# Two steps of a chunked recurrence at a time between the weight tiles of a projection

## The reference

```
z = rmsnorm(h); q, f, i, og, pool, gates = split(z @ w_in)
f = lb + (1 - lb) * sigmoid(f);  k = 1 - f;  a = cumsum(log f) in a chunk
o_inter = (q * exp(a)) @ S                      # S: state of the head, 128 x 64
scores[t, s] = sum_k q[t] * exp(a[t] - a[s]) * k[s],  s <= t
o = o_inter + scores @ v
S = exp(a_last) * S + (k * exp(a_last - a))^T @ v
```

## Time and profile before

| | us |
|---|---|
| median of 3 runs | 1472.34 |
| profiled execution, its own time | 1473.41 |
| span of the profile | 1471.6 |
| TensorE matmuls busy | 1451.9 |
| VectorE busy | 828.5 |
| ScalarE busy | 691.1 |
| GpSimd busy | 161.6 |

### The profile page before, as it was taken

One profiled execution on the slowest core, in us unless ns is written; L12 is line 12 of the kernel. 1 busy time (PEld: TensorE's weight loads), 2 busy tenths in 40 slices (PEclk: granted clock), 3 DMA queues, 4 the chain that ended last, 5 costly groups with the idle time before them and its releaser, 6 DMA issues.

```text
span 1471.6 us, 26477 instructions
## 1 busy us (share of the span) xinstructions
PE 1451.9 (99%) x11311; PEld 1284.0 (87%) x11311; DVE 828.5 (56%) x1335; ACT 691.1 (47%) x1025; POOL 161.6 (11%) x308
## 2 busy tenths in 40 slices
PE   7999999999999999999999999999999999999998
PEld 7999989999999898998888777788899888778888
DVE  6487867764656556654335787642223566644343
ACT  6475877853443222322233676642222777743232
POOL 0025400000000000000000044300000233320000
PEclk9999999999999999999999999999999999999999
DMA  7222121123422223222334333433223333342222
GB/s 238 94 66 89 63 83 59 59 73 137 131 94 86 87 87 113 87 87 82 106 101 108 63 47 20 77 94 109 86 86 89 68 71 71 72 105 93 86 94 79
DMA packets 138968, 130.24 MB, mean 89 GB/s; under 512 B 26569, under 2 KB 134884, under 8 KB 138596
## 3 DMA queue, kind: packets, MB, share of 16 engines
q1 hardware_dynamic: 134084, 120.39, 26.0%
q0 software_dynamic: 4752, 8.16, 5.3%
q10 hardware_dynamic: 16, 0.00, 0.0%
HBM read 119.69 MB, written 4.26 MB: 84 GB/s over the span
## 4 chain that ended last, share of the span: by engine, by line
PE 91%; DVE 3%; ACT 3%; issue 1%; DMA 0%; SPq 0%; DVEq 0%; ACTq 0%
PE PS L962 79%; PE PS L1288 3%; PE PS L1261 2%; PE PS L1244 2%; DVE wlo L1937 1%; PE PS L1248 1%; PE PS L1247 1%; PE PS L1073 1%; ACT L1439 1%; ACT whi L1439 0%; DMA xt<-in_x 0%; ACT Pm L1439 0%; PE PS L1129 0%; PE PS L1029 0%; DVE zlo L1985 0%
## 5 line engine op out<-in xcount | busy, mean ns | idle before, releaser
L962 PE MATMUL PS<-zhi,whi 128*128 128x258 f32 (+2 forms) x1856 | 486.9, 320 | 3.2 <-ACT qf L1439 1.0
L962 PE MATMUL PS<-zhi,wlo 128*128 128x258 f32 (+2 forms) x1856 | 476.8, 314 | 0.0
L962 PE MATMUL PS<-zlo,whi 128*128 128x258 f32 (+2 forms) x1856 | 475.4, 314 | 0.6 <-DVE zlo L1985 0.6
L962 PEld LDWEIGHTS PS<-zhi,whi 128*128 128x128 f32 x1856 | 306.9, 189 | 27.9 <-issue 2.6
L962 PEld LDWEIGHTS PS<-zhi,wlo 128*128 128x128 f32 x1856 | 305.6, 189 | 22.3
L962 PEld LDWEIGHTS PS<-zlo,whi 128*128 128x128 f32 x1856 | 305.5, 189 | 20.8 <-DVE zlo L1985 0.8
L1937 DVE TENSOR_TENSOR wlo<-raw,whi 128x2048 fp32r<-128x2048 f32 (+2 forms) x114 | 249.3, 2187 | 121.5 <-ACT whi L1439 121.4
L1439 ACT ACTIVATE whi<-raw 128x2048 fp32r<-128x2048 f32 (+2 forms) x114 | 207.4, 1820 | 150.4 <-DMA raw<-in_w_up 55.2
L1439 ACT ACTIVATE Pm<-Pm,small 128x144 f32<-128x144 f32 (+3 forms) x128 | 73.1, 571 | 38.6 <-DVE small L2467 38.3
L2467 DVE CUSTOM_DVE_ANT_0 Pm<-PS,cmask 128x144 f32<-128x144 f32 (+3 forms) x128 | 62.9, 503 | 35.8 <-PE PS L1244 21.5
L962 PE MATMUL PS<-glo,whi 128*128 128x512 f32 x176 | 69.9, 397 | 0.0
(11 more groups left out here) (357 smaller groups left out, 2171.4 us busy)
## 6 DMA issues: line engine op xcount, KB each, us to landing
raw<-in_w_in SPq DMA_DIRECT2D x50, 1024.0 KB, 5.3
raw<-in_w_up SPq DMA_DIRECT2D x22, 1024.0 KB, 5.1
raw<-in_w_out SPq DMA_DIRECT2D x8, 1024.0 KB, 5.2
raw<-in_w_down SPq DMA_DIRECT2D x8, 1024.0 KB, 5.3
raw<-in_w_br_mla SPq DMA_DIRECT2D x4, 1024.0 KB, 5.1
raw<-in_w_br_fox SPq DMA_DIRECT2D x4, 1024.0 KB, 5.1
raw<-in_w_down SPq DMA_DIRECT2D x4, 768.0 KB, 4.3
hspill<-hT SPq DMA_DIRECT2D x1, 2112.0 KB, 7.6
```

The lines of the kernel that those rows point to most:

```text
L962: ins = mm(o_, l_, r_, start=first, stop=last)
```

## The change

Three things. On TensorE, steps 1, 3 and 5 of a pair are not done behind their own weight tile but kept in a list `held`, and done with the next entry of the order that does not itself end in such a step; on that occasion the held step and the entry's own follow each other. The update of chunk c goes to columns 128 c to 128 c + 127 of bank 7, so only the update of chunk 2 still waits for a state. On VectorE, `state(c)` waits for the updates of both steps of a couple, and reads the new columns; of the two places where differences and state were taken ahead, the one for i = 3 (in the f tile with i = 2) stays and the one for i = 4 goes back to its own entry.

```diff
@@ TensorE, step
-                        else:
-                            pe.wait_ge(s_ready, 4 * p + c)
+                        elif c == 2:
+                            pe.wait_ge(s_ready, 4 * p + 2)
                         for hh in range(2):
                             h = 2 * p + hh
+                            u0 = P * c + 64 * hh
                             for r in range(0, P, 32):
-                                ins = mm(PS[r:r + 32, 7, 64 * hh:64 * hh + 64], kdt[0:n, hh, c, r:r + 32],
+                                ins = mm(PS[r:r + 32, 7, u0:u0 + 64], kdt[0:n, hh, c, r:r + 32],
                                          vtok1[0:n, c, 64 * h:64 * h + 64], start=True, stop=True)
@@ TensorE, order
-            waiting = []
+            waiting, held = [], []
...
-                for p, i in steps:
+                held += [(p, i) for p, i in steps]
+                if steps and steps[-1][1] in (1, 3, 5):
+                    continue
+                for p, i in held:
                     rec_step(p, i)
+                held = []
@@ VectorE, state
-                    dve.wait_ge(upd_done, 4 * p + c + 1)
+                    dve.wait_ge(upd_done, 4 * p + c // 2 * 2 + 2)
...
-                                                     in1=PS[:, 7, 64 * hh:64 * hh + 64], op0=ALU.mult, op1=ALU.add)
+                                                     in1=PS[:, 7, P * c + 64 * hh:P * c + 64 * hh + 64], op0=ALU.mult, op1=ALU.add)
@@ VectorE, order
-                    ahead = i in (3, 4) and p < 3
+                    ahead = i == 3 and p < 3
...
                         rec_step(p_, i_ + 1, "products")
+                    if i_ == 2:
                         rec_step(p_, i_ + 1, "state and differences")
```

## The result

The changed kernel takes 1480.72 us, the median of 4 runs (1480.12 to 1481.32); the kernel before takes 1472.38 beside it. The ratio is 1.0057 (95% interval 1.0044 to 1.007): slower by 8.3 us, where 3.8 was forecast, and outside the range of the forecast (1473.4 to 1479.0). The profiled execution has a span of 1479.5, 7.9 longer. No instruction came or went; TensorE is as busy as in the earlier trace rows.

What follows compares the result with a forecast made beforehand. TensorE, busy 99%, was taken as the bound. Joins -1.36, chain +3.04, ("pool", 1) +1.09, GpSimd +0.7 and +0.2, slot +1.1, given back -1.0 made +3.8: 1472.34 + 3.8 = 1476.1 us, range 1473.4 to 1479.0.

Steps and rivals of the forecast that it cites:

- Joins: TensorE's recurrence visits: seven clean joins of two steps save 0.194 us each, -1.36 together.
- Rival (d): Joined visits save nothing, since the second step refills the array as a weight tile would; 1477.5 us, chance 0.06.
- Chain before step 4: Pairs 0 to 2: late state(0) delays products 4; +1.16, +1.16, +0.72 us. N is the start of t(3)'s matmuls.
- ("pool", 1): Pair 1's second pool tile waits for its slot: +1.09 us, +0.7 for GpSimd. M is the end of products 4.
- Slot of t(4) in pair 2: ScalarE frees the slot of the weight tile beside step 4 late for t(6): +1.1 us.
- Given back: The old 1.1 us wait ahead of pair 1's last step mostly goes: -1.0 us, bounds 0 and 1.1.
- (a): Rival: the chain before step 4 fits, no new wait arises and old waits go; 1469.7 us, chance 0.06.
- (b): Rival: only the wait before step 4 comes, the slots are free in time; 1473.6 us, chance 0.16.
- GpSimd in pair 0: Pooling beside VectorE at steps 5 to 7 delays products 6 and 7: +0.2 us, bounds 0 and 1.9.
- Rival (c): GpSimd's cost to VectorE is at its upper bounds, +1.1 and +1.7 us more; 1478.9 us, chance 0.12.

Runs made afterwards that it cites:

- x1: The changed kernel with VectorE's differences 3 and 5 put before the state update in their entries; 1475.05 us, ratio 1.001 to the kernel before.
- x4: Against the kernel before, only steps 1 and 2 joined, in pairs 0, 1 and 3, differences and state ahead as before; 1475.81 us, ratio 1.0021.
- x5: The changed kernel without GpSimd's window sums, means and differences (pooled inputs are plain copies); 1475.82 us, ratio 1.0023 to the full kernel before.
- second profile: The changed kernel run and profiled once more, nothing altered; 1481.65 us, ratio 1.0062 to the kernel before.
- x3: Against the kernel before, only steps 5 and 6 joined, in pairs 0, 2 and 3, differences ahead as before; 1471.98 us, ratio 0.9993.
- x11: The changed kernel with differences first, step 5 of pair 1 behind its own tile, and 128 already-met waits ahead of TensorE's first tile; 1479.15 us, ratio 1.0042.
- x14: The kernel before with pair 3's three joins, 5+6 of pair 2, and 1+2 of pairs 0 and 1 with differences first there; 1471.33 us, ratio 0.999.

## Why the prediction was wrong in size

The direction, the chain and the place of every wait but the holes were right; the sum was 4.5 us short. The step that failed is the price of GpSimd's work beside VectorE, 0.7 + 0.2 for what cost 1.7 + 1.96, and a term that was not there, the clock behind the waits. By its own steps:

- **Joins.** Forecast -0.194 each. 1+2 saves 0.18 in pair 0 and 5+6 saves 0.26, 3+4 of pair 3 some 0.4 (13.57 from tile to tile for 14.03). Rival (d) is out, and pair 3 gained 0.82 for 0.58.
- **Chain before step 4.** Forecast waits of 1.35 and a next tile at N + 15.20; 1.22 and N + 15.17 in pair 0, 14.17 behind N in pair 1, 1.32 in pair 2. Right, and its mechanism is shown by both `x1` (head removed, waits gone) and `x4` (this join alone brings it). In pair 1 the wait was 0.81, in part since a hole of 0.24 stood in the tile ahead of it.
- **("pool", 1).** Forecast 1.55 + 0.7 for GpSimd: 2.25. It was 2.23, and that is luck: two errors of 1 us cancel. The slot was forecast free at M + 9.9 with GpSimd and came at M + 10.9 (M is 162.85); TensorE was forecast there at M + 7.7 and came at M + 8.8, for the most part because of the hole in the visit (0.79). The 9.2 without GpSimd is right: `x5` has M + 9.87, of which 0.66 is what the copies add to differences 5. So GpSimd's part was 1.7 for 0.7, near the upper bound of 1.8; in the second profile it was 0.35 (M + 9.55).
- **Slot of t(4) in pair 2.** Forecast 1.1, was 1.0. **Given back:** forecast 1.0, was 1.15. Rivals (a) and (b) are out.
- **GpSimd in pair 0, the step that failed most.** "products 6 and 7 have 1 to 2 us to spare: bounds 0 and 1.9, taken 0.2, near the lower since the pooling's first 7 us cost VectorE little before." It was 1.96. The spare time was right: 1.67 in `x5`. The contention was 3.7 us of VectorE's, and 3.7 less 1.67 is the wait. The rows of before had most of it: after those first 7 us the second pooling begins, and beside it the weight half and differences 7 took 3.41, 1.57 and 1.57 for 2.27, 0.69 and 0.69 (above), 2.9 us more. It cost no time then, as products 7 were 3.24 us early all the same. `x5` shows that without GpSimd's sums nothing is left of the wait. `x3`, which also puts the differences of level 5 back ahead, has none either; which share each of the late chain, the moved differences and the held step has is not separated. Rival (c) had both of GpSimd's costs, at 12%, and came to 1478.9. Its reading of the port, by which an instruction can be held for the rest of the other engine's, is the one that the rows bear out.
- **The clock, not in the sum.** Two waits of about 2 us were in reach of the forecast, one of them in so many words, and I took a wait to cost its own length. Behind them TensorE ran at 1.2 GHz for some 3.4 us: 1.4 each, 2.8 in the profiled execution. It comes in some executions only: the second profile has one of the two. What it adds to the median is not shown; the four timed runs took 1481.29 and 1480.14 at a mean clock of 0.997, and 1481.32 and 1480.12 at 0.999.
- **The hole, not in the sum.** The joined visit of pair 1 is the place where a block of instructions comes late. As far as the order tells, it cost nothing here: it stands ahead of ("pool", 1), whose slot came 2.23 after TensorE did, so without the hole that wait would be longer by as much. This is argued; `x11`, where the same exchange is seen at step 5, bears it out. In the kernel before, with the visits apart, packets start at 146.8 and 161.1 and no hole follows; that a weight tile between two visits gives the fetch its time is argued, not tried by itself.

The three that were missing, 1.76 in pair 0, 1.0 at the slot of ("pool", 1) and 2.8 of clock, make 5.6 and stand against 8.9 - 3.8 = 5.1 in the profiled execution; the joins' 0.3 and the 0.15 more given back make up the difference. What stays open: why the same wait brings the lower clock in one execution and not in the next, and how much of the median is clock.

## What to carry to other kernels

Before two small steps are merged, ask what is queued behind the first one's result on the other engines: 0.19 us a visit was won and 1.2 lost, because the state update stood ahead of the differences in VectorE's order. Where it stood behind them (`x14`, steps 1+2), merging brought no wait. When a chain gets late, look in the old trace for the delays that its slack has hidden so far: here 2.9 us of contention with GpSimd stood there in full, at no cost, 3.24 us ahead of need. And a wait of 1.3 us or more on TensorE can cost about 1.5 on top in clock.

## What the runs showed of the hardware

- Within the recurrence, the granted clock fell to 0.50 in five places of eighteen profiles, each time 0.2 to 1.6 us behind the end of a wait of 1.3 to 2.5 us, and came back to 1.00 after some 3.4 us; it cost 1.4 to 1.6 us. Waits of 1.3, 2.0 and 2.5 us were also followed by 1.00.
- TensorE can outrun its instruction stream: in a joined visit of 168 small matmuls, one every 11 ns (1.85 us), the next one came 2.3 to 2.7 us behind the start of a 16 KB packet on the instruction queue. With a wait ahead of it the hole is shorter (0.79 behind 0.81, 1.80 behind none), and it can hide a wait that lies behind it.
- Two-input fp32 instructions of VectorE on 128 x 512 take 0.69 alone and 0.9 to 1.8 beside GpSimd; a 128 x 2048 one 2.27 and 3.40. They and GpSimd's instructions end in turn: where GpSimd adds, subtracts or converts, a held one of VectorE's ends 0.55 behind GpSimd's last.
